# The order of the expert units in a two-layer diffusion step: one-expert units behind all two-expert units

## What is computed

```python
def swiglu(x, wg, wu, wd):
    return (jax.nn.silu(x @ wg) * (x @ wu)) @ wd
...
    _, idx = lax.top_k(masked, TOP_K)                      # 6 of 64 experts for each token
    wts = jnp.take_along_axis(scores, idx, axis=1)
    wts = wts / (jnp.sum(wts, axis=-1, keepdims=True) + 1e-20) * ROUTED_SCALE
    return routed_experts(x, idx, wts, w_gate, w_up, w_down) + swiglu(x, s_gate, s_up, s_down)
```

## Time and profile before

| | |
|---|---|
| runs | 2812.24, 2799.26, 2817.89 us; median 2812.24 |
| profiled execution | 2817.59 us, span of its instructions 2816.0 us |
| TensorE matmul busy | 2175.8 us, 77% of the span |
| weight loads of TensorE | 1493.1 us, 53% |
| VectorE, ScalarE, GpSimd busy | 30%, 13%, 11% |
| moved by DMA | 571.21 MB, mean 203 GB/s |
| expert weights | 3 x 128 transfers of 1 MiB |
| mean granted TensorE clock | 0.857 |

### The profile page before, as it was taken

How to read it: one execution, slowest core, us unless ns; L and a number is a source line. 1 busy time by engine, 2 the same in 40 slices (tenths; PEclk the granted TensorE clock), 3 DMA queues, 4 the chain that set the end, 5 groups by cost and what they waited for, 6 DMA issues and landing times.

```text
span 2816.0 us, 37208 instructions
## 1 busy us (share of the span) xinstructions
PE 2175.8 (77%) x15513; PEld 1493.1 (53%) x15513; DVE 835.2 (30%) x1628; ACT 357.0 (13%) x803; POOL 321.5 (11%) x380
## 2 busy tenths in 40 slices
PE   5987788888488888889837981957767889888982
PEld 2445566666465555556513440647655556556651
DVE  1123433333332111111132317265544111111114
ACT  0002222111011111111100000211101111111110
POOL 0000132222001111111100000013200111111110
PEclk9995687777789999999978985568887999999996
DMA  7551111111125999999980220000002699999994
GB/s 290 194 194 34 60 61 61 65 61 61 49 82 190 415 392 398 407 399 398 399 319 30 99 82 0 23 1 2 9 4 114 237 416 403 402 392 401 398 382 186
DMA packets 122403, 571.21 MB, mean 203 GB/s; under 512 B 26353, under 2 KB 30065, under 8 KB 70769
## 3 DMA queue, kind: packets, MB, share of 16 engines
q1 hardware_dynamic: 85392, 496.07, 44.8%
q0 software_dynamic: 26624, 56.67, 5.3%
q10 hardware_dynamic: 10208, 15.95, 1.6%
HBM read 564.36 MB, written 46.20 MB: 217 GB/s over the span
## 4 chain that ended last, share of the span: by engine, by line
PE 51%; DMA 26%; DVE 13%; issue 3%; ACT 1%; ACTq 1%; PEld 1%; PEldq 1%; SPq 1%; POOL 0%; DVEq 0%; POOLq 0%
PE bank L570 47%; DMA ring<-in_exp_w_up 16%; DVE arena L1595 8%; DMA ring<-in_exp_w_down 5%; DMA ring<-in_exp_w_gate 2%; DMA mixed<-choice_rows 2%; DVE arena L1612 2%; PE bank L710 1%; PEld bank L570 1%; ACTq L1244 1%; PE bank L1130 1%; DVE mixed L1595 1%; PEldq L641 1%; ACT arena L1232 1%; DMA ring<-in_ev_w_in 1%
## 5 line engine op out<-in xcount | busy, mean ns | idle before, releaser
L570 PE MATMUL bank<-ring,arena 128*64 128x256 f32 (+3 forms) x5168 | 878.6, 435 | 149.5 <-DMA ring<-in_exp_w_up 60.3
L570 PEld LDWEIGHTS bank<-ring,arena 128*64 128x64 f32 (+1 forms) x5168 | 531.0, 150 | 445.1 <-issue 353.5
L570 PE MATMUL bank<-arena 64*64 64x64 f32 (+9 forms) x6260 | 451.5, 258 | 49.0 <-DVE arena L1595 33.6
L570 PEld LDWEIGHTS bank<-arena 64*64 64x64 f32 (+3 forms) x6260 | 391.2, 164 | 92.1 <-issue 52.5
L1609 DVE COPY arena<-bank 128x512 f32<-128x512 f32 (+3 forms) x291 | 153.5, 532 | 949.8 <-PE bank L570 559.5
L570 PE MATMUL bank<-ring,hT 128*128 128x512 f32 (+2 forms) x672 | 268.9, 561 | 30.4 <-DVE hT L1600 18.5
L2279 POOL TENSOR_TENSOR arena<-arena,consts 64x256 f32<-64x256 f32 x216 | 161.0, 745 | 1098.7 <-DVE arena L1595 573.9
L570 PEld LDWEIGHTS bank<-ring,hT 128*128 128x128 f32 x672 | 128.0, 198 | 170.7 <-issue 146.4
L2293 POOL DMA_INDIRECT choice_rows<-arena x76 | 76.3, 1005 | 708.4 <-DVE arena L1609 708.4
L2287 POOL DMA_INDIRECT arena<-token_rows,arena x76 | 77.6, 1021 | 632.1 <-DVE arena L1599 601.6
L570 PE MATMUL bank<-hT,ring 128*128 128x384 f32 x384 | 127.5, 493 | 20.8 <-ACT hT L1472 20.0
(11 more groups left out here) (155 smaller groups left out, 1319.3 us busy)
## 6 DMA issues: line engine op xcount, KB each, us to landing
ring<-in_exp_w_gate SPq DMA_DIRECT2D x128, 1024.0 KB, 10.3
ring<-in_exp_w_up SPq DMA_DIRECT2D x128, 1024.0 KB, 11.5
ring<-in_exp_w_down SPq DMA_DIRECT2D x128, 1024.0 KB, 11.9
ring<-in_mod_w SPq DMA_DIRECT2D x48, 1024.0 KB, 8.3
ring<-in_od_w_in SPq DMA_DIRECT2D x14, 1024.0 KB, 7.4
arena<-choice_rows POOLq DMA_DIRECT2D x4, 3072.0 KB, 14.2
ring<-in_ev_w_in SPq DMA_DIRECT2D x10, 1024.0 KB, 7.5
ring<-in_ev_w_out SPq DMA_DIRECT2D x4, 1024.0 KB, 5.9
```

The costliest lines, as they stand in the source:

```text
L570: return nc.tensor.matmul(out, lhsT, rhs, start=start, stop=stop, **kw)
```

## The change

The loop that builds the list of units places a pair at each step but the last ten, and a single at those. The result: units 0 and 1 as before, units 2 to 27 the 26 pairs, units 28 to 37 the singles of ranks 2 to 11. All else follows from the list: the order of the pieces on SP, of the gathers and scatters on POOL, and of the matmuls. The number of instructions of each kind does not change.

```diff
     units, big, pair = [(0,), (1,)], FIXED, BIG
     spread = (EXPERTS - BIG) // 2 + BIG - FIXED
     for i in range(spread):
-        if (i + 1) * (BIG - FIXED) // spread > i * (BIG - FIXED) // spread:
+        if i >= spread - (BIG - FIXED):
             units.append((big,))
             big += 1
         else:
```

## The result

| | before | after |
|---|---|---|
| median of the runs taken side by side | 2809.51 us (2799.26 to 2817.89) | 2846.30 us (2842.83 to 2851.14) |
| profiled execution | 2817.59 us | 2842.83 us |
| expert stage, mark of unit 0 to mark of unit 37, layer 0 | 542.48 us | 558.63 us |
| the same, layer 1 | 543.99 us | 562.58 us |
| from mark 37 of layer 0 to mark 0 of layer 1 | 781.62 us | 772.36 us |

The account below looks back on a forecast made before the run. The two expert stages bound the kernel, PE pacing singles and DMA pairs behind pairs. Stages +33.0 and +30.9 us, less 2.5 behind layer 0's last mark, gave +61.4; from 2812.24 us that predicted 2873.6 us, range 2842 to 2905.

Parts of the forecast that it names:

- The turn of a single in a row: Ten singles ending each expert stage: 12.6 + 7 x 12.4 + 2 x 11.7 = 122.8 us, PE busy throughout.
- The turn of a pair in a row: Units 5 to 27 of each stage: 17.2 us a pair, bounds 16.1 and 17.75, 23 pairs 395.6 us.
- Rival A: Row of pairs runs at 421 GB/s, 16.1 us a turn: +11 us, 2823 us; chance 0.13.
- The last scatter: Behind the last mark of layer 0, it lands sooner: 2.5 us off, between nothing and 3.5; layer 1 0.
- rival B: PE's clock falls in the row of pairs; low for 0.7 of a turn, +181 us, 2993 us; chance 0.10.
- Mechanism: In the stages, singles let the ring run ahead for the next pair; nine pairs lose 13.75 for 17.2, 31 us.
- those fourteen turns: Layer 0 before the change, pairs behind pairs: 237.42 us, 16.96 each, at 389 GB/s, DMA setting the pace.

Follow-up runs that it names:

- e4: Changed order, with gathers from unit 2 on bringing almost no token rows: 2809.95 us, ratio 0.9987 to the kernel before the change.
- e5: Changed order, with four matmuls added to each unit's gate step (they appear as eight): 2892.37 us, ratio 1.0282 to the kernel before the change.
- e1: Against the kernel before the change, all twelve singles stand first, then the 26 pairs in a row: 2850.89 us, ratio 1.0136.
- e3: Against the kernel before the change, five pairs and two singles in turn, five times, then the remaining pairs: 2815.13 us, ratio 1.0006.
- e6: Against the kernel before the change, nine pairs, five singles, nine pairs, five singles, eight pairs: 2829.45 us, ratio 1.0064.

## Why the forecast had the sign right and the size wrong

Point by point, by the terms of the sum.

- *The turn of a single in a row*: 122.8 us forecast for ten, 120.18 and 120.19 measured. The single's picks add nothing in a row of singles (12.11 against 12.09 for unit 1 before); I had added 0.3. That is 5.2 us of the error.
- *The turn of a pair in a row*: this step failed. I took 17.2 us, because pairs behind pairs ran at 389 GB/s before, and read the low rate as that of a ring run empty. Measured: 16.58 and 16.75, at 409 GB/s in layer 0, and from unit 14 on mostly 16.2 at 409 to 418, with PE waiting for every piece. So a row of pairs does not run at the low rate merely because its ring is empty. 23 x 0.62 = 14.3 us in layer 0 and 23 x 0.45 = 10.4 in layer 1 are the greater part of the error, 24.7 us. Rival A had said just this of the rate, and at 16.1 us it came within 0.1 of most turns from unit 14 on; but the eight pairs from unit 5 to unit 12, with more token rows (0.64 to 0.51 MB a turn), took 17.1, so the total fell between the forecast and A. e4 shows the token rows' part in it: without half of them the turn falls by 0.8 us on average.
- *The last scatter*: 2.5 us off forecast, 2.1 measured.
- *The clock* (rival B): in layer 0 none of the 23 turns reads under 1.00, in layer 1 three do (0.81, 0.91, 0.90). The long row of pairs did not bring more of them than the earlier trace rows had. The three are not free: units 23 to 27, which hold them, take 85.7 us in layer 1 and 81.6 in layer 0, more than the 3.8 us by which layer 1's row is longer. Part of it is no matter of the clock: the turn at 0.81 begins with a wait of 3.0 us for gate weights. Nor does a PE that is merely busier cost it: in e5 1.8 us more of PE in a pair's turn moves nothing.
  The Trainium skill, TensorE: Matmul & The Clock Gate, section "HAM oscillation — how this bites in real kernels", tells of a loop that waits for data longer than it works on a tile, and whose clock falls at each tile. That is not the case here: PE waited two or three times in most of the 46 turns, but 1.05 to 1.38 us at a time in the turn shown above, against 3.65 us and more of work behind each wait, and the clock fell in three of them.
- *Mechanism*: right, by e1 and e3. A single costs PE a full turn and DMA only half a pair's; the spread order hands the spare DMA time to the next pair, a long row of singles cannot. The size that the ring gives back per block was argued from turns, and e6's loss fits it only in part.

With the measured terms the sum closes: +16.2 and +18.6 in the stages, -2.1 behind the first, 32.7 us, against 35 by the ratio.

Two things stay open. Why the second and third pair behind a single ran at 389 GB/s before, and pairs from unit 14 on at 409 to 418 in a row, with full engines, was not settled. The queues narrow it down: an average weight packet, 7.27 to 7.28 KB in both, took 0.297 us in those fourteen turns and 0.282 in units 14 to 21 of the changed kernel (estimates from the weight queue's share of 16 engines' time and its packets, layer 0), so each packet was slower before. The place behind a single is not the cause by itself, since in layer 0 of e3 the third and fourth pair behind a block ran at 402 to 422 GB/s, the fifth at 372 to 413. And a deeper ring, which by this account would let longer rows of singles pass without loss, was not tried.

## What to carry to other kernels

Where two kinds of work have different limits, price the order by the slower resource's idle time: here a single takes 12.1 us of PE and 3.63 MB / 409 GB/s = 8.9 us of DMA, so 3 us of DMA are lost for each one that the buffers' lead (two singles here, some 5 us given back behind them) can't take up. A mean rate taken from turns that follow each other irregularly is not the rate of a steady row; bound it by the best rate seen too, and let the size of the forecast follow. Idle time of the engine that does not set the pace is free: filling half of PE's 3.6 us in a turn of 16.2 cost nothing there (e5).

## Not expected

The steady turns of pairs are the same to a few hundredths of a microsecond and come in steps: 15.6 us (e4), 16.2 and 16.8 (most kernels here), while the token rows of successive units fall steadily. In the changed kernel units 14 to 21 all take 16.16 to 16.21 us in layer 0, with 0.48 MB of rows in the first of these turns and 0.37 in the last. The runs do not say what makes the steps.
